# Attention values in a hybrid decoder layer: V as TensorE's weights, probabilities scaled before the transpose

## What is computed

```python
def hybrid_layer(x, ...):
    h = rmsnorm(x, norm_g)
    proj = jnp.einsum('bsd,de->bse', h, w_in)
    ... = jnp.split(proj, IN_OFFSETS, axis=-1)
    y_lru = rglru_group(lru_u, lru_z, ...)     # conv, gates, linear scan, times silu(z)
    y_nsa = nsa_group(nsa_q, ...)              # 8 heads of 64, 2 key/value heads
    y_fox = fox_group(fox_q, fox_k, fox_v, ...)  # 8 heads of 64
    y = jnp.concatenate([y_lru, y_nsa, y_fox], axis=-1)
    return x + jnp.einsum('bse,ed->bsd', y, w_out)

# nsa_group:
    o = g[..., 0:1] * o_cmp + g[..., 1:2] * o_slc + g[..., 2:3] * o_win
    return o.reshape(bsz, seq, NSA_WIDTH) * jax.nn.silu(z)

# fox_group, for a block of queries:
    s = q k^T * ATTN_SCALE + c_q - c_k         # c: cumulated log forget gates
    p = safe_softmax(s, s_pos <= t)
    o = p v                                    # then times silu(z)
```

## Time and profile before

| | |
|---|---|
| median of 3 runs | 488.44 us (488.08 to 489.48) |
| the profiled execution | 488.75 us |
| span in the profile | 486.6 us |
| mean granted TensorE clock | 0.989 |
| TensorE busy | 466.6 us, 96% |
| TensorE weight loads | 383.0 us, 79% |
| VectorE busy | 320.7 us, 66% |
| ScalarE busy | 250.1 us, 51% |
| GpSimd busy | 16.8 us, 3% |
| TensorE's share of the chain that ended last | 81% |

### The profile page before, as it was taken

The page is one execution under the profiler, slowest core; times in us unless marked ns, Lnnn a source line. Parts: engine busy times, 40 slices in busy tenths (PEclk is TensorE's granted clock), DMA queues, the critical chain, the costliest instruction groups (busy, mean ns, idle before and its releaser), DMA issues.

```text
span 486.6 us, 7134 instructions
## 1 busy us (share of the span) xinstructions
PE 466.6 (96%) x2632; PEld 383.0 (79%) x2632; DVE 320.7 (66%) x584; ACT 250.1 (51%) x472; POOL 16.8 (3%) x25
## 2 busy tenths in 40 slices
PE   5899999999779999999999999999999999899997
PEld 2576777778668799999987797888799987688885
DVE  4977479877977978878736873757966547722204
ACT  4656684767354765555517874851655535312200
POOL 3012230000000000000000000000000000000000
PEclk9999999999959999999999999999999999999999
DMA  7732234431121200000002224461300002742004
GB/s 253 289 95 79 92 83 131 119 96 50 71 97 43 88 0 2 1 2 2 0 1 88 80 71 153 109 195 44 129 2 2 1 1 86 288 144 86 1 0 172
DMA packets 12961, 39.55 MB, mean 81 GB/s; under 512 B 1792, under 2 KB 2048, under 8 KB 12672
## 3 DMA queue, kind: packets, MB, share of 16 engines
q1 hardware_dynamic: 12928, 39.11, 24.7%
HBM read 32.81 MB, written 2.10 MB: 72 GB/s over the span
## 4 chain that ended last, share of the span: by engine, by line
PE 81%; DVE 12%; ACT 3%; issue 2%; DMA 1%; POOL 0%; SPq 0%; DVEq 0%; ACTq 0%
PE bank L1058 10%; PE bank L1060 10%; PE bank L1059 10%; PE bank L1167 10%; PE bank L1153 6%; PE bank L1282 4%; PE bank L1284 4%; PE bank L1283 4%; PE bank L1141 4%; PE bank L1145 3%; DVE wl L713 2%; PE bank L1069 2%; PE bank L1195 2%; PE bank L1038 2%; PE bank L1040 2%
## 5 line engine op out<-in xcount | busy, mean ns | idle before, releaser
L1058 PE MATMUL bank<-xh,wh 128*128 128x512 f32 (+1 forms) x264 | 113.6, 430 | 0.0
L1060 PE MATMUL bank<-xh,wl 128*128 128x512 f32 (+1 forms) x264 | 105.2, 398 | 0.0
L1059 PE MATMUL bank<-xl,wh 128*128 128x512 f32 (+1 forms) x264 | 104.7, 396 | 0.0
L713 DVE TENSOR_TENSOR wl<-raw,wh 128x1024 fp32r<-128x1024 f32 x51 | 63.1, 1241 | 32.6 <-ACT wh L447 32.1
L447 ACT ACTIVATE wh<-raw 128x1024 fp32r<-128x1024 f32 x51 | 53.2, 1049 | 34.0 <-PE bank L1284 33.2
L555 ACT ACTIVATE probs<-bank,negmax 128x128 f32<-128x128 f32 (+1 forms) x96 | 50.2, 526 | 37.5 <-DVE negmax L905 30.6
L905 DVE TENSOR_REDUCE negmax<-bank 128x1 f32<-128x128 f32 (+1 forms) x96 | 45.7, 488 | 25.2 <-PE bank L1145 23.3
L1059 PEld LDWEIGHTS bank<-xl,wh 128*128 128x128 f32 (+1 forms) x264 | 49.7, 188 | 15.1 <-issue 3.9
L1058 PEld LDWEIGHTS bank<-xh,wh 128*128 128x128 f32 (+1 forms) x264 | 49.8, 189 | 15.0 <-issue 4.0
L1060 PEld LDWEIGHTS bank<-xh,wl 128*128 128x128 f32 (+1 forms) x264 | 49.6, 188 | 12.7
L1153 PE MATMUL bank<-cst,probs 128*128 128x128 f32 x240 | 42.5, 275 | 1.0 <-ACT probs L555 1.0
(11 more groups left out here) (198 smaller groups left out, 770.3 us busy)
## 6 DMA issues: line engine op xcount, KB each, us to landing
raw<-in_w_in SPq DMA_DIRECT2D x39, 512.0 KB, 3.4
raw<-in_w_out SPq DMA_DIRECT2D x12, 512.0 KB, 3.5
x_raw<-in_xT SPq DMA_DIRECT2D x8, 256.0 KB, 6.9
x_res<-in_x_tok SPq DMA_DIRECT2D x1, 2048.0 KB, 8.6
out_y<-y_out SPq DMA_DIRECT2D x8, 256.0 KB, 2.1
cmp_w_sb<-in_cmp_w SPq DMA_DIRECT2D x1, 1024.0 KB, 10.6
kh_fox<-kh_fox SPq DMA_DIRECT2D x8, 128.0 KB, 2.4
kl_fox<-kl_fox SPq DMA_DIRECT2D x8, 128.0 KB, 2.4
```

Source lines behind the costliest of these rows:

```text
L713: dve.tensor_tensor(wl[:, c % HL, :], raw[:, c % RAW, :], wh[:, c % HL, :].bitcast(F32), ALU.subtract).then_inc(wl_ready, 1)
L1058: pe.matmul(dst, hi, xh[:, k, :], start=(k == 0), stop=False)
L1059: pe.matmul(dst, hi, xl[:, k, :], start=False, stop=False)
L1060: mm = pe.matmul(dst, lo, xh[:, k, :], start=False, stop=(k == KT - 1))
```

## The change

- Value matmuls swap their operands: V's 128x64 block is the weights, the transposed probabilities are streamed, for all query blocks that see this key block at once (512, 384, 256 or 128 columns). The output is feature-major. Two heads form a pair: the even head's output goes to PSUM partitions 0 to 63, the odd head's to 64 to 127 of the same bank.
- Units go by pairs: even head and odd head of t = 0, of t = 1, and so on. A pair's values are computed in four steps, one for each key block, behind the pair's eight units (`V_LAG` + 8 units after the unit's scores). `pT` holds two pairs.
- The normalisation can't follow the values any more, since queries are no longer on partitions. VectorE now takes the reciprocal for two units, and multiplies each unit's `probs` by it and by the branch gate (a vector of ones for fox), in place in SBUF, before the transposes. `T_LAG` is 4; `P_RING` is 5, with `work` as the fifth buffer.
- NSA's two branches are summed in PSUM; VectorE adds the result to `o_nsa` once for both branches of a pair of heads. In fox it copies it to `o_fox`.
- The output transposes (`o_transposed`) go, as do their waits; `z_times_o` reads `o_nsa` or `o_fox` from SBUF.
- The mask matmul is fp32r instead of bf16. The compressed branch's values are feature-major too: four matmuls of 128 columns instead of two of 256.

```diff
-T_LAG, V_LAG = 3, 5
-S_RING, P_RING, PT_RING, M_RING = 4, 4, 3, 8
+T_LAG, V_LAG = 4, 5
+S_RING, P_RING, M_RING, R_RING = 4, 5, 8, 4
+KEYS = 3 * P
+PT_W = (NT - 1) * KEYS + NT * P
...
-        ident_b = sb("ident_b", [P, P], BF16)
-        mask_b = sb("mask_b", [P, P], BF16)
+        ident_r = sb("ident_r", [P, P], F32R)
+        mask_r = sb("mask_r", [P, P], F32R)
...
-                    probs = sb("probs", [P, P_RING, SEQ], F32, w)
-                    pT = sb("pT", [P, PT_RING, SEQ], F32, w)
+                    o_fox = sb("o_fox", [P, HEADS // 2, SEQ], F32, w)
+                    probs = sb("probs", [P, P_RING - 1, SEQ], F32, w)
+                    pT = sb("pT", [P, 2, 2, PT_W], F32, w)
...
             elif k >= 0:
                 eng.wait_ge(proj_done, proj_units(k + 1))
-        heads = [("nsa", h, b) for h in range(HEADS) for b in (1, 2)] + [("fox", h, 0) for h in range(HEADS)]
-        NSA_UNITS, UNITS = 2 * HEADS * NT, len(heads) * NT
+        pairs = [("nsa", i, b) for i in range(HEADS // 2) for b in (1, 2)] + [("fox", i, 0) for i in range(HEADS // 2)]
+        PAIR_UNITS = 2 * NT
+        NSA_UNITS, UNITS = HEADS * PAIR_UNITS, len(pairs) * PAIR_UNITS
+
+        def unit(u):
+
...
+        def wait_pT_buffer(eng, u):
+
+            w = u // PAIR_UNITS
+            if w >= 2:
+                eng.wait_ge(av_done, NT * (w - 1))
+
+        def probs_of(u, a, b):
+
+            slot = u % P_RING
+            return work[:, a:b] if slot == P_RING - 1 else probs[:, slot, a:b]
+
+        def pT_of(u):
+
+            t = unit(u)[3]
+            return pT[:, u // PAIR_UNITS % 2, u % 2, t * KEYS:t * KEYS + (t + 1) * P]
         def steps(first, last):
-            return [(s, (lambda u: u if first <= u < last else None)) for s in range(first, last + V_LAG + 2)]
+            return [(s, (lambda u: u if first <= u < last else None)) for s in range(first, last + V_LAG + PAIR_UNITS)]
+
+        def values_step(first, last, s):
+
+            w, r = divmod(s - V_LAG - PAIR_UNITS, PAIR_UNITS)
+            return (w, r // 2) if r % 2 == 0 and first <= w * PAIR_UNITS < last else None
...
+                if q >= R_RING:
+                    act.wait_ge(rcp_ready, q - R_RING + 1)
                 n = (t + 1) * P
-                act.activation(probs[:, u % P_RING, 0:n], SCORE[u % S_RING][:, 0:n], ACT.Exp,
+                act.activation(probs_of(u, 0, n), SCORE[u % S_RING][:, 0:n], ACT.Exp,
                                bias=negmax[:, u % M_RING:u % M_RING + 1],
-                               accum_out=rsum[:, v % 3, t:t + 1]).then_inc(p_ready, 1)
+                               accum_out=rsum[:, q % R_RING, u % 2:u % 2 + 1]).then_inc(p_ready, 1)
...
-                    dst = by_token(z)
-                dve.tensor_tensor(dst, by_token(z), o, ALU.mult).then_inc(y_ready, 1)
-
-            def finish_head(v):
-                group, h, b = heads[v]
-                dve.wait_ge(av_done, NT * (v + 1))
-                if v >= 1:
-                    dve.wait_ge(head_done, v)
-                link(dve.reciprocal(rcp[:, 0, :], rsum[:, v % 3, :]))
-                o = OUT[v % 2][:, 0:NT * HD].rearrange("p (t d) -> p t d", t=NT)
+                    dve.tensor_tensor(z, z, o_fox[:, i - 4, :], ALU.mult).then_inc(y_ready, 1)
+
+            def scale_probs(u):
+                group, h, b, t = unit(u)
+                p = probs_of(u, 0, (t + 1) * P)
+                gate = gates[:, t, 3 * h + b:3 * h + b + 1] if group == "nsa" else one1[:, :]
+                dve.tensor_scalar(p, p, rcp[:, u // 2 % R_RING, u % 2:u % 2 + 1], gate,
+                                  ALU.mult, ALU.mult).then_inc(p_scaled, 1)
+
+            def finish_pair(w):
+                group, i, b = pairs[w]
+                if b == 1:
+                    return
+                dve.wait_ge(av_done, NT * (w + 1))
+                o = OUT[out_of(w) % 2][:, :]
                 if group == "nsa":
-                    if v == 0:
+                    if i == 0:
                         dve.wait_ge(cmp_o_read, NT)
-                    link(dve.tensor_tensor(rcp[:, 0, :], rcp[:, 0, :], gates[:, :, 3 * h + b], ALU.mult))
-                    scaled = head_out[:, :].rearrange("p (t d) -> p t d", t=NT)
-                    link(dve.tensor_tensor(scaled, o, rcp[:, 0, :].unsqueeze(2).broadcast_to([P, NT, HD]), ALU.mult))
-                    acc = o_nsa[:, :, h * HD:(h + 1) * HD]
-                    dve.tensor_tensor(acc, acc, scaled, ALU.add).then_inc(head_done, 1)
+                    dve.tensor_tensor(o_nsa[:, i, :], o, o_nsa[:, i, :], ALU.add).then_inc(pair_done, 1)
                 else:
-                    dve.tensor_tensor(o_fox[:, :, h * HD:(h + 1) * HD], o,
-                                      rcp[:, 0, :].unsqueeze(2).broadcast_to([P, NT, HD]),
-                                      ALU.mult).then_inc(head_done, 1)
+                    dve.tensor_copy(o_fox[:, i, :], o).then_inc(pair_done, 1)
             def attention(first, last):
...
                         dve.wait_ge(pT_ready, u + 1)
-                        if u >= PT_RING:
-                            dve.wait_ge(av_done, u - PT_RING + 1)
-                        dve.tensor_copy(pT[:, u % PT_RING, 0:n], PT[u % PTB][:, 0:n]).then_inc(pT_dve, 1)
-                    u = inside(s - V_LAG - 1)
-                    if u is not None and u % NT == NT - 1:
-                        finish_head(u // NT)
+                        wait_pT_buffer(dve, u)
+                        dve.tensor_copy(pT_of(u), PT[u % PTB][:, 0:n]).then_inc(pT_dve, 1)
+                    u = inside(s - 1)
+                    if u is not None and u % 2:
+                        q = u // 2
+                        dve.wait_ge(p_ready, u + 1)
+                        if q >= R_RING:
+                            dve.wait_ge(p_scaled, 2 * (q - R_RING) + 2)
+                        dve.reciprocal(rcp[:, q % R_RING, :], rsum[:, q % R_RING, :]).then_inc(rcp_ready, 1)
+                        dve.wait_ge(rcp_ready, q + 1)
+                        for x in (u - 1, u):
+                            scale_probs(x)
+                    v = values_step(first, last, s - 1)
+                    if v is not None and v[1] == NT - 1:
+                        finish_pair(v[0])
...
+                for i in range(HEADS // 2):
+                    g, r = divmod(i, GROUP // 2)
+                    mm = pe.matmul(OUT[t % 2][:, i * P:(i + 1) * P], v_blocks[:, g, r * P:(r + 1) * P],
+                                   std[:, g * P:(g + 1) * P], start=True, stop=True)
                 mm.then_inc(cmp_o, 1)
             def unit_scores(u):
-                v, t = divmod(u, NT)
...
-                pe.matmul(dst[:, t * P:n], ident_b[:, :], mask_b[:, :], start=False, stop=False)
-                if heads[v][0] == "fox":
-                    pe.matmul(dst[:, 0:n], head_sel[:, heads[v][1], :], c_parts[:, 0:n], start=False, stop=False)
+                pe.matmul(dst[:, t * P:n], ident_r[:, :], mask_r[:, :], start=False, stop=False)
+                if group == "fox":
+                    pe.matmul(dst[:, 0:n], head_sel[:, h, :], c_parts[:, 0:n], start=False, stop=False)
                 pe.matmul(dst[:, 0:n], q, kl[:, 0:n], start=False, stop=True).then_inc(s_ready, 1)
             def unit_transpose(u):
-                pe.wait_ge(p_ready, u + 1)
+                pe.wait_ge(p_scaled, u + 1)
                 if u >= PTB:
                     wait_pT(pe, u - PTB)
-                for j in range(u % NT + 1):
+                for j in range(unit(u)[3] + 1):
                     cols = slice(j * P, (j + 1) * P)
-                    mm = pe.transpose(PT[u % PTB][:, cols], probs[:, u % P_RING, cols], ident)
+                    mm = pe.transpose(PT[u % PTB][:, cols], probs_of(u, j * P, (j + 1) * P), ident)
                 mm.then_inc(pT_ready, 1)
-            def unit_values(u):
-                v, t = divmod(u, NT)
-                wait_pT(pe, u)
-                if t == 0 and v >= 2:
-                    pe.wait_ge(head_done, v - 1)
-                elif t == 0:
-                    pe.wait_ge(cmp_o_read, NT - 1 + v)
-                if t == 0 and v in (2 * HEADS, 2 * HEADS + 1):
-                    pe.wait_ge(y_ready, 3 + v % 2)
-                val = values_of(u)
-                for j in range(t + 1):
-                    mm = pe.matmul(OUT[v % 2][:, t * HD:(t + 1) * HD], pT[:, u % PT_RING, j * P:(j + 1) * P], val[:, j, :],
-                                   start=(j == 0), stop=(j == t))
+            def pair_values(w, j):
+
+                group, i, b = pairs[w]
+                o = out_of(w)
+                if j == 0:
+                    for u in range(w * PAIR_UNITS, (w + 1) * PAIR_UNITS):
+                        wait_pT(pe, u)
+                    if b != 2:
+                        if o >= 2:
+                            pe.wait_ge(pair_done, o - 1)
+                        else:
+                            pe.wait_ge(cmp_o_read, NT - 1 + o)
```

(12 more changed lines are left out.)

## The result

The changed kernel takes **494.65 us** (median of 4 runs, 493.20 to 495.16) beside 488.76 us for the kernel before on the same chip (4 runs, 488.08 to 489.48): a ratio of 1.0117, 95% interval 1.0096 to 1.0139. The profiled execution of after took 495.08 us with a span of 493.3, against 486.6 before.

A forecast was written before the change was run, and what follows sets the result against it. TensorE was taken to bound both attention stages, VectorE and ScalarE the last 20.4 us. NSA -2.6, fox -0.3 and output transposes -0.4 sum to -3.3 us: median 485.2, own range 482.5 to 488, with rivals 481.5 to 495.

The forecast's parts named there:

- Value matmuls, 3.3 us a pair instead of 4.2: Attention's value matmuls on TensorE: partly overlapping halves take 3.3 us a pair, bounds 2.2 and 4.4, against 4.2 before.
- TensorE's need, 8.9 and 10.0 us: TensorE's time per pair after the change: 8.9 us in NSA (8.7 to 9.3), 10.0 in fox.
- So I price a switch at nothing: Changes between 64-column and 128-column weights on TensorE cost nothing, read from the fg chunk.
- VectorE's need, 8.5 to 9.3 and 9.0 to 9.8 us: VectorE's time per pair in NSA and fox, with scalings at 2.8 us and up to 0.8 given back by overlap.
- I take 9.5 us a pair for NSA and 10.2 for fox: Pair times in attention; eight and four pairs plus 1.2 us of lag give NSA -2.6 and fox -0.3 with tails.
- Transposes of the output, -0.4 (up to 1.7): Removed output transposes: one set ahead of the zn-chunk chain counts, -0.4 us, up to 1.7 with slack; last stage nothing.
- Tails +0.9 each: Value matmuls behind the projections of NSA and fox: 2.6 us instead of 1.7.
- No overlap (494): Rival 1: the two heads' value matmuls don't overlap, +5.5 us, 494; chance 0.25.
- A price for each change of tile (494.5): Rival 3: a drain of 0.15 to 0.17 us at each change, 1.4 us a pair, 494.5; chance 0.10.
- Rival 2: The loop's waits set the rate in attention: pairs of 10.0 and 10.8 us, +3.1, 491.5 us; chance 0.17.
- Rival 4: All goes together: pairs of 9.0 and 9.9 us, 480.5 us; chance 0.10.
- wrong if TensorE idles for scaled probabilities: One of three signs given in advance that would show the prediction wrong; no size.

The follow-up runs named there:

- Experiment 1: Changed kernel with VectorE's scalings left out, transposes waiting for the exponential instead: 478.56 us, ratio 0.9782.
- 8: Changed kernel with three VectorE steps of other stages moved out of the first NSA and fox pairs: 490.37 us, ratio 1.0038.
- experiment 9: Changed kernel with one-pointer scalings, every second one on ScalarE, idle transposes in the zf chunks, three VectorE steps moved out of first pairs: 482.63 us, ratio 0.9875.
- Experiment 3: Changed kernel with four idle 128x128 transposes of a constant behind each of the four zf chunks: 491.63 us, ratio 1.0038.
- two near-twins: Kernel before with the mask matmul in fp32r (488.84 us), and kernel before with the last LRU output moved to NSA's drain (488.76 us).
- experiment 2: Changed kernel with both heads of a pair writing PSUM partitions 0 to 63, through the same array columns: 512.7 us, ratio 1.0487.
- first control: Kernel before with the last LRU output (1.4 us of VectorE) moved from step 16 to NSA's drain: 488.76 us, ratio 1.0003.

## Why the prediction was wrong, point by point

- **Value matmuls, 3.3 us a pair instead of 4.2.** Both sizes were too large. The halves do overlap, but wholly and not by a quarter, two and two starting together. The four sizes of step (1.01, 0.80, 0.59, 0.37) grow by 0.21 us per 128 columns, which is one head's stream alone (0.86 / 4); the streams are the forecast's lower bound of 2.15, and 0.15 us a step come on top. After: 2.8 a pair. Before, by its timeline:

```profile
211.21 0.78 PE L1167 MATMUL bank<-v_nsa,pT 128*128 128x64 f32 x6
211.80 0.31 PE L1141 MATMUL bank<-kh_nsa,q_nsa 128*128 128x128 f32 x1
...
212.37 1.00 PE L1167 MATMUL bank<-v_nsa,pT 128*128 128x64 f32 x8
213.18 0.36 PE L1141 MATMUL bank<-kh_nsa,q_nsa 128*128 128x256 f32 x1
```

  0.59 us for six and 0.81 for eight instructions, with 0.37 and 0.14 for four and two 1.9 a head, 3.8 a pair and not 4.2. The two errors cancel: the matmuls save 1.0 us a pair (0.9 forecast), counted from the start of a value step to the next score. The four changes into the value steps, 0.4 us, are in the rest of the step.
- **TensorE's need, 8.9 and 10.0 us.** Measured 9.13 and 10.06 with the scalings gone. What the forecast missed is the rest of its step (10.09 - 3.8 = 6.3, not 5.9) and the mask (0.3 taken; 0, and 0.15 lost in fox). "So I price a switch at nothing" was wrong too: at 0.09 us a change it is 0.7 us a pair.
- **VectorE's need, 8.5 to 9.3 and 9.0 to 9.8 us.** Measured 9.12 and 9.4. A head's scalings were sized at 1.4 us and take 0.34 + 0.41 + 0.48 + 0.54 = 1.8, 3.5 a pair and not 2.8. With them the sum is 10.0; what brings it down to 9.1 is that neighbours overlap, as the forecast had allowed for: without the scalings VectorE is 6.28 us busy a pair, so they add 2.84.
- **"I take 9.5 us a pair for NSA and 10.2 for fox", times eight and four, plus 1.2.** This is the step that failed. Fox's steady 10.11 is right; NSA's steady 9.83 is 0.33 above the 9.5, 2.6 us over eight pairs. Worse is that eight times a steady pair plus 1.2 us is not the stage: the second, the third and the last pair take 11.81, 11.13 and 14.46. Of the 6.8 us between the forecast's -3.5 and the measured +3.3, 4.2 lie there, and all 2.6 us of fox's. Experiment 1 shows that the scalings bring it (9.2, 9.2 and 12.0 without them), 8 and 9 that a part is other stages' VectorE work in those pairs. In the last pair TensorE waits again and again for scalings and copies of VectorE (5.08 us busy in the 6.57 from its last score to the projection). The rest is in part the clock: every profile in which NSA's second pair takes 11.5 us or more has 3.4 us at half clock within it, and the two without it are shorter (10.5 in experiment 9, 9.2 in experiment 1). How the second pair's 11.8 us and fox's first divide between waiting and half clock wasn't separated.
- **The output projection**, which the forecast didn't mention: +2.5 us. It put the transposes that the change takes off TensorE in the zf chunks at nothing ("none of it counts"); they did count, for the clock. TensorE was busy 16.05 us of 20.4 there (17.96 of 20.3), and the clock stood at 0.69 in the next 10 us: some 6 of them at half, 1.2 GHz. Experiment 3 gives it back. The kernel before has the same loss in part (72.5 in two near-twins), so the change made it larger and regular rather than new.
- **Transposes of the output, -0.4 (up to 1.7).** -0.9 to fox's first maximum. TensorE reaches fox's first score 2.1 us sooner by the same count, and then waits for the same VectorE chain of 13.8 us.
- **Tails +0.9 each, finish +0.1, last chain unchanged.** 0.7, 0.75, 0.1: right.
- **The rivals.** No overlap (494) is refuted by experiment 2: with it the kernel takes 512.7, and the forecast's own rival was too cheap, for the reasons given there. A price for each change of tile (494.5) is half true: it is there, at 0.09 us and not 0.15 to 0.17, but TensorE's need is 9.13 us a pair and not that rival's 10.3. The Trainium skill (TensorEngine Tiling (Array Packing), Key Properties) says that different tiles run in parallel, and the traces agree (1.01 for 1.86 us). It also says that changing the tiling mode drains the engine; the traces agree in that each change here costs 0.09 us, though the fg chunk's 64-column weights show no such step, and why they don't is open. That 494.65 is close to both rivals' times is chance. Rival 2, the waits of the loop, is the one that came true in kind: 10.0 a pair was too high for the steady ones (9.83) and too low for the ends, and its 491.5 us lack the output projection's 2.5. (Rival 4's terms give 480.0 and not 480.5.) The sentence "wrong if TensorE idles for scaled probabilities" names what happened.

## What to carry to other kernels

A change that trades TensorE time for VectorE time, with both then above 90% busy, wins less than the steady period says. Work out the first and last iterations one by one, with what other stages left in them, and look for an engine with room (ScalarE here, 5.7 of 9.8 us) before counting the gain. And TensorE work that is taken out of a stretch bound by others is not free to remove: read the granted clock behind it.

## What the runs showed of the hardware

- Two fp32 matmuls with 64-column weights each, on different columns of the array and different halves of PSUM's partitions, start within 0.01 us of each other and run wholly side by side: 1.01 us for both at 512 streamed columns, 1.86 through the same half.
- A change from 128-column to 64-column weights or back costs 0.09 us: 0.20 instead of 0.11 us from a transpose to the next start, 0.52 instead of 0.43 behind a 512-column stream, the same in experiments 1, 2 and 9. The fp32r weights of the fg chunk don't show it (0.23 us to the next start, as within the chunk).
- A VectorE scaling in SBUF by two per-partition operands takes 0.06 us more than by one at 128, 256, 384 and 512 columns alike (344, 411, 478, 544 ns against 284, 349, 419, 484).
- The half clock at the start of the output projection comes and goes between kernels that are alike to 0.1% in time and in what TensorE did: in the first 10 us of it 43 matmuls at full clock in the kernel before, 36 at 0.83 in the first control, with TensorE 2.6 us busy in the 5 us ahead of it in both.
